# Rotary keys carried in the rows of the cache pages, and copied to their partitions by GpSimd

## The reference

```
s_past = (q_lat . ckv_past + q_rope . kr_past) * ATTN_SCALE     # 16 heads, 4096 positions
p      = softmax([s_past, s_new])
o      = p[past] . ckv_past + p[new] . c_kv
```

## Time and profile before

| | us |
|---|---|
| median of 3 runs | 932.12 (930.16 to 932.34) |
| the profiled execution | 928.51 |
| its span | 926.8 |
| TensorE busy in it | 885.7 (96%) |
| VectorE busy | 482.8 (52%) |
| ScalarE busy | 247.0 (27%) |
| GpSimd busy | 145.5 (16%) |

### The profile page before, as it was taken

How to read it: one execution, slowest core, us unless ns; L and a number is a source line. 1 busy time by engine, 2 the same in 40 slices (tenths; PEclk the granted TensorE clock), 3 DMA queues, 4 the chain that set the end, 5 groups by cost and what they waited for, 6 DMA issues and landing times.

```text
span 926.8 us, 14793 instructions
## 1 busy us (share of the span) xinstructions
PE 885.7 (96%) x5217; PEld 531.5 (57%) x5217; DVE 482.8 (52%) x1093; ACT 247.0 (27%) x553; POOL 145.5 (16%) x242
## 2 busy tenths in 40 slices
PE   8999999999999999999999999899999889987997
PEld 6777777777777766556678545443333333333443
DVE  2343789978752267767666445761111211114784
ACT  1122221122244126656620111221111111002246
POOL 0423433434323000000000000011211101111000
PEclk9999999999999999999999999999999989999999
DMA  9977998999999520101341695639999999998601
GB/s 371 379 246 253 332 337 281 332 358 327 321 307 340 206 75 26 44 21 43 114 193 46 250 422 217 260 118 410 423 423 423 422 422 426 422 418 347 236 24 69
DMA packets 76178, 247.61 MB, mean 267 GB/s; under 512 B 15397, under 2 KB 22830, under 8 KB 67110
## 3 DMA queue, kind: packets, MB, share of 16 engines
q1 hardware_dynamic: 54422, 191.42, 53.8%
q0 software_dynamic: 16288, 35.29, 10.6%
q10 hardware_dynamic: 5392, 19.93, 6.0%
HBM read 240.98 MB, written 18.05 MB: 279 GB/s over the span
## 4 chain that ended last, share of the span: by engine, by line
PE 76%; DMA 13%; DVE 5%; ACT 2%; issue 2%; SPq 1%; DVEq 0%; ACTq 0%; POOLq 0%
PE ps L1068 12%; DMA arena<-in_wexp 10%; PE ps L1572 9%; PE ps L1019 8%; PE ps L1492 6%; PE ps L1416 4%; PE ps L1594 3%; PE ps L1127 3%; PE ps L1157 3%; PE ps L1242 3%; PE ps L1059 3%; PE ps L1697 2%; PE ps L1264 2%; PE ps L1206 2%; PE ps L1223 2%
## 5 line engine op out<-in xcount | busy, mean ns | idle before, releaser
L1068 PE MATMUL ps<-arena 128*128 128x260 f32 x544 | 125.4, 386 | 2.1 <-DMA arena<-in_xT 1.5
L1068 PEld LDWEIGHTS ps<-arena 128*128 128x128 f32 x544 | 101.4, 190 | 23.0 <-issue 4.5
L2118 DVE SCALAR_TENSOR_TENSOR arena<-arena,vec 128x512 f32<-128x512 f32 x120 | 81.8, 746 | 0.0
L1019 PE MATMUL ps<-arena 128*128 128x260 f32 x336 | 78.5, 387 | 0.1
L1594 PE MATMUL ps<-arena 128*64 128x512 f32 x288 | 68.0, 615 | 6.2 <-DMA arena<-in_wexp 6.2
L2989 POOL DMA_DIRECT2D arena<-in_kv x96 | 52.1, 544 | 132.5 <-issue 128.6
L2814 DVE TENSOR_TENSOR arena<-ps,arena 128x256 f32<-128x256 f32 x18 | 7.6, 425 | 124.1 <-ACT arena L1967 124.1
L1572 PE MATMUL ps<-arena 128*64 128x512 f32 x288 | 65.4, 608 | 4.8 <-DMA arena<-in_wexp 3.8
L1019 PEld LDWEIGHTS ps<-arena 128*128 128x128 f32 x336 | 62.1, 190 | 12.9 <-issue 3.7
L1572 PE MATMUL ps<-arena,con 128*64 128x512 f32 x288 | 64.0, 596 | 3.3 <-DMA arena<-in_wexp 3.3
L1492 PE MATMUL ps<-arena 128*128 128x512 f32 x128 | 58.0, 600 | 0.0
(11 more groups left out here) (424 smaller groups left out, 1363.7 us busy)
## 6 DMA issues: line engine op xcount, KB each, us to landing
arena<-in_wexp SPq DMA_DIRECT2D x26, 2048.0 KB, 27.0
arena<-in_kv SPq DMA_DIRECT2D x160, 256.0 KB, 8.7
arena<-in_wexp SPq DMA_DIRECT2D x36, 1024.0 KB, 27.7
arena<-in_kv POOLq DMA_DIRECT2D x96, 256.0 KB, 7.4
arena<-in_w ACTq DMA_DIRECT2D x35, 512.0 KB, 8.5
arena<-in_wexp SPq DMA_DIRECT2D x16, 512.0 KB, 8.6
arena<-in_wo SPq DMA_DIRECT2D x8, 512.0 KB, 4.7
arena<-in_w_out SPq DMA_DIRECT2D x4, 1024.0 KB, 7.6
```

What stands on the lines that cost most here:

```text
L1019: y = mm(ps[:, paired_bank(p, n), 0:TH], left(k), right(k), start=(k == 0), stop=(k == KD // 2 - 1))
L1068: y = mm(ps[:, b + h, 0:TH], w[:, k], xT[:, k, h * TH:(h + 1) * TH], start=(k == 0), stop=(k == KD - 1))
L2118: y = v.scalar_tensor_tensor(out=aT[:, c, 0:NPR], in0=win, scalar=wt, in1=aT[:, c, 0:NPR], op0=ALU.mult, op1=ALU.add)
```

## The change

The keys no longer have a tensor of their own. They lie in the page's rows, between the transposed and the plain latents, as 32 more floats a row: `REC` is 544 floats, 2176 bytes. In a page the keys of positions 32c to 32c + 31 stand in partitions 32c to 32c + 31, so that a page fills all 128 partitions, with the 32 values of a key along them. All key transfers are gone from SP and GpSimd, and SP's wait on `s_ks` with them.

The score matmuls contract over 128 partitions that hold four groups. For this, GpSimd copies a step's keys from `kvr` to `krr` with four copies, each 64 partitions of 256 floats; x chooses the half that is written, h the half that is read. The copies of step n wait until all 16 pages of the step have landed. GpSimd's order is now: copy the keys of step n-1, wait for `v_step` n-2, ask for six pages of step n. `k_step` waits for the four copies in front of its key matmuls, and these write their 128 columns in runs of 32 to all of the step's columns. `krr` is now a tensor beside the arena, which keeps its size, and the descriptor scratch of the program is set to 4096 bytes a partition.

```diff
-REC = 2 * P + KVL
+REC = 2 * P + P // 4 + KVL
...
-A_KR = A_KV + 2 * STEPS * REC
-A_END1 = A_KR + 2 * 4 * P
+A_END1 = A_KV + 2 * STEPS * REC
...
-        krr = at(A_KR, 2 * 4 * P).rearrange("p (s b n) -> p s b n", s=2, b=4)
+        krr = sb("krr", [P, 2 * 4 * P])[:].rearrange("p (s b u h i) -> p s b u h i", s=2, b=4, u=2, h=2)
...
             sp.wait_ge(s_con, 112)
             step_pages(0)
-            step_keys(0)
-            step_keys(1)
             sp.wait_ge(s_q4, 1)
             step_pages(1)
             for n in range(2, STEPS):
...
-                sp.wait_ge(s_ks, n - 1)
-                step_keys(n)
                 sp.wait_ge(s_vs, n - 1)
                 step_pages(n)
...
-                pe.wait_ge(s_kv[s], 32 * SPN * (n // 2 + 1))
-                pe.wait_ge(s_kvp[s], 32 * (STEPS - SPN) * (n // 2 + 1))
+                pe.wait_ge(s_kv[s], 16 * SPN * (n // 2 + 1))
+                pe.wait_ge(s_kvp[s], 16 * (STEPS - SPN) * (n // 2 + 1))
...
+                pe.wait_ge(s_kf, 4 * (n + 1))
                 for j in range(2):
                     for bb in range(4):
-                        y = mm(ps[32 * bb:32 * bb + 32, bank, j * P:(j + 1) * P], qrz[:, j, 4 * r + bb, :], krr[:, s, bb],
-                               start=False, stop=(j == 1))
+                        y = mm(ps[32 * bb:32 * bb + 32, bank, 0:2 * P].rearrange("p (u h j i) -> p j u h i", u=2, h=2, j=2)[:, j],
+                               qrz[:, j, 4 * r + bb, :], krr[:, s, bb], start=False, stop=(j == 1))
...
-                                   kvr[:, s, bb, 2 * x + u, 2 * P:REC], start=(u == 0), stop=(u == 1))
+                                   kvr[:, s, bb, 2 * x + u, 2 * P + 32:REC], start=(u == 0), stop=(u == 1))
...
             def step_keys(n):
-                pool.load(numbers, pages[0:1, STEPS * n + SPN:STEPS * (n + 1)])
-                for j in range(STEPS - SPN):
-                    pg = pool.snap(numbers[j], min_val=0, max_val=NPOOL - 1)
-                    pool.dma_start(page_keys(n, SPN + j), a["kr"][bass.ds(pg, 1)].rearrange("a p n -> (a p) n")
-                                   ).then_inc(s_kvp[n % 2], 16)
+
+                pool.wait_ge(s_kv[n % 2], 16 * SPN * (n // 2 + 1))
+                pool.wait_ge(s_kvp[n % 2], 16 * (STEPS - SPN) * (n // 2 + 1))
+                for x in range(SIDES):
+                    for h in range(2):
+                        gp.tensor_copy(krr[64 * x:64 * x + 64, n % 2, :, :, h],
+                                       kvr[64 * h:64 * h + 64, n % 2, :, 2 * x:2 * x + 2, 2 * P:2 * P + 32]).then_inc(s_kf, 1)
 
             pool.wait_ge(s_con, 112)
             step_pages(0)
-            step_keys(0)
-            step_keys(1)
             pool.wait_ge(s_q4, 1)
             step_pages(1)
+            step_keys(0)
             for n in range(2, STEPS):
-                pool.wait_ge(s_ks, n - 1)
-                step_keys(n)
+                step_keys(n - 1)
                 pool.wait_ge(s_vs, n - 1)
                 step_pages(n)
+            step_keys(STEPS - 1)
...
-    krT = ckr.transpose(0, 2, 1)
+    krT = ckr.reshape(NPOOL, 4, 32, ROPE).transpose(0, 1, 3, 2).reshape(NPOOL, P, 32)
...
-        "kv": np.concatenate([ckT, ckv], 2), "kr": krT,
+        "kv": np.concatenate([ckT, krT, ckv], 2),
...
-    nc = bacc.Bacc("TRN2", target_bir_lowering=False, num_devices=1)
+    nc = bacc.Bacc("TRN2", target_bir_lowering=False, num_devices=1, dynamic_dma_scratch_size=4096)
```

More of the change, by code:

```diff
@@ L704, in decoder_layer @@
         OV_SLOT, OV_LOADS = 0, sum(k % 3 == 0 for k in range(EPAIRS))
-        def page_keys(n, j):
-            b, u = divmod(j, 4)
-            return krr[32 * u:32 * u + 32, n % 2, b]
         def narrow(bank, rows, w, ready=None):
@@ L1233, in scores @@
                 if hh == 0:
-                    pe.wait_ge(s_kf, 4)
+                    pe.wait_ge(s_kf, 4 * STEPS + 4)
                     pe.wait_ge(s_cse, 1)
```

## The result

| | before | after |
|---|---|---|
| median of 22 runs, us | 929.77 (927.52 to 932.46) | 932.30 (929.88 to 935.18) |
| ratio after / before | | 1.0025 (95% interval 1.0014 to 1.0035) |
| span of the profiled execution, us | 926.8 | 930.5 |
| TensorE busy from 76 to 310 us, of 234 | 231.64 | 229.25 |

The change makes the kernel 2.3 us slower (0.0025 x 929.8; 1.3 to 3.3 by the interval). The forecast was +1.2 us, inside 0.3% of no change, and that is where the result lies. The median of before is 929.77 over 22 runs, where the three that the prediction had gave 932.12, so only the ratio is compared. All ratios here are of runs in the chip's fast state: one of the four executions of e7 (2601.86 us, its cause unknown) and one of the kernel before beside e11 and e12 (950.42 us) are left out.

What follows compares the result with a forecast made beforehand. It took TensorE and just-in-time pages to bound the cache steps. Terms of -0.3 (SP's queue), +0.2 (copies), +0.8 (GpSimd's wait) and +0.5 (busy VectorE) gave +1.2 us, 933.3 us, with a range of 929.5 to 946.

Steps and rivals of the forecast that it cites:

- What bounds the kernel: Cache steps, 76 to 310 us: TensorE and DMA nearly full, pages just in time, 0.0 to 3.3 us margin a step.
- The bytes: Page and key transfers: same 0.26 MB a step in fewer transfers, net 0; bounds -0.8 and +0.8 us a step.
- Rival C: DMA queues relieved of small transfers, TensorE's 2.36 us of idle time go: 929.8 us; over 0.3% faster, chance 0.10.
- SP's queue: SP loses 160 issues and its `s_ks` waits; step 8's pages asked for 3.0 us sooner; -0.3 us.
- GpSimd's copies: At each step's landing: four copies of 356 ns, 1.42 us, against 1.55 us of cover; +0.2 us in all.
- copies that meet a busy VectorE: GpSimd's copies in the cache steps: now and then they meet a busy VectorE; +0.5 us.
- GpSimd's wait: GpSimd's page requests move back 4.8 us behind the landing, last page 0.3 us later a step; +0.8 us in all.
- The key matmuls and the scratch: `k_step`'s matmuls writing in runs of 32: 0; smaller scratch holding GpSimd's requests back: a rival, +370 us, chance 0.02.
- Rival A: GpSimd's circle of request, landing, copies sets the step, 14.5 to 17.5 us a turn; up to +12.4 us, 944.5; chance 0.18.
- Rival B: GpSimd's copies wait out VectorE's taps, 4.4 us for four; +6.5 us, 938.6; chance 0.20.
- The signs: In the cache steps: rival B by copies of 0.7 us and more; forecast by at most 3.5 us waits ahead of `k_step`'s matmuls.

Runs made afterwards that it cites:

- e7: Against the changed kernel: every step's four copies are made twice and `k_step` waits for both sets; 1.0154 of the kernel before.
- e11: Against the changed kernel: ScalarE makes the copies, ahead of its waits for VectorE's sums, and GpSimd neither copies nor waits for landings; second measurement, 0.9997 of the kernel before.
- e12: The changed kernel as it is, measured again beside the kernel with ScalarE's copies; 1.0015 of the kernel before.
- e1: Against the changed kernel: no GpSimd copies and no wait for a landing, krr zeroed once, cached rotary keys left out; 0.9979 of the kernel before.
- e2: Against the changed kernel: the four copies gone, GpSimd's wait for the landing kept, cached rotary keys left out; 1.0000 of the kernel before.
- e8: Against the kernel before: only the descriptor scratch set to 4096 bytes a partition; 1.0019.
- e10: Against the kernel before: only the descriptor scratch set to 4096 bytes a partition, measured a second time; 0.9985.
- e4: Against the changed kernel: SP asks for all sixteen pages of a step and GpSimd only copies keys; 1.0010 of the kernel before.
- e3: Against the changed kernel: each copy is a memset of the same places, which reads no SBUF, with the same waits; 0.9993 of the kernel before.
- e6: Against the changed kernel: GpSimd asks for its six pages before it copies the previous step's keys; 1.0358 of the kernel before.

## Why the prediction was right, and where its sum was off

**What bounds the kernel**: right. Pages that land just in time set what TensorE loses, and 3.2 of the 3.7 us between the two profiles lie ahead of `k_step` 15, in the stretch that was read.

**The bytes**: 0 was right for the time (e1). The engines' busy share fell by 0.06 of 234 us, so the transfers were relieved, but no wait of TensorE went with it; e1 has even 2.9 us of them. Rival C had its mechanism and no price.

**SP's queue**: right in kind. SP asks for step 8's pages 1.2 us after `v_step` 6 instead of 4.2, but `v_step` 6 itself ends 2.1 us later (its `k_step` was the one with the waits above), so they leave at 176.25 instead of 177.17.

**GpSimd's copies**: the two terms of them (0.2 and 0.5) came out very differently. Undisturbed, a copy took 0.40 us where 0.356 had been worked out, and four took 1.77 with their gaps, not 1.42. But the cover was 1.75 us and not 1.55, and the key matmuls followed 0.05 us after the copies, not 0.2. The errors cancel, and the forecast's 0.1 us in a step without margin stands as 0.03 in step 14. The mis-sized term is the 0.5 us booked for copies that meet a busy VectorE. It had no working, and it stood for copies of 612 ns in the mean and for all of the 2.3 us that the key matmuls waited, in steps 3, 6 and 12.

**GpSimd's wait**: booked at +0.8, the largest term of the sum, measured at 0 to within 0.16% of the kernel before (e2; beside e1 up to 2.7 us stay open). Both of its parts were too dear. The 2.12 us between `v_step` and the first request were taken over whole behind the copies; it is 0.27 us or nothing there. The requests for steps 2 to 15 leave 5.0 us after `v_step` in the mean instead of 2.1, which is 2.9 us later and not 4.8. And GpSimd's pages did not become the last in every step: the copies of step 6 begin with SP's landing, and those of step 9 with GpSimd's, whose last request left at 200.7 and landed 10.3 us later, at 211.0, with the copies at 211.12.

**The key matmuls and the scratch**: 0, right. The 16 records of a step still take 0.62 to 0.65 us; e8 and e10 together give 1.000.

**Rival A** got the picture and not the cause. The circle is what the chain shows, and `k_step`s in the changed kernel stand (313.00 - 95.19) / 13 = 16.75 us apart, GpSimd's copies just as far. But e2 keeps the circle and loses nothing against the kernel before, and e4 breaks it and still has 2.1 us of waits for copies. A chain through it says what came last, not what a shorter wait would be worth.

**Rival B** is the mechanism that is there, at a third of its price (2.3 of 6.5 us). Four copies had been priced at 4.4 us; beside taps and other instructions with two operands they took 2.5 to 3.2, and 5.7 once. They were held up in ten steps, but seven of these had room: in steps 4, 7 to 11 and 13 the copies began 1.5 to 4.9 us ahead of `k_step`, where the margins that had been read in the kernel before were 0.0 to 3.3. What made this room wasn't separated; e3, whose key matmuls never wait, has 4.7 us of it in step 4 and 2.7 in step 8. B was refused the forecast for want of a row. The Trainium skill's rule ("SBUF — State Buffer", "Who interferes with whom") had it: the trace agrees, with 402 ns in the median and up to 4310 ns beside VectorE's two-operand taps, and e3 agrees with its further part, that an instruction of GpSimd that only writes isn't held up. The rule should have given B the larger chance. It wouldn't have given a better number: B's +6.5 us is farther from the +2.3 measured than the forecast's +1.2.

**The signs** that the prediction had named point to B as well: copies of 0.7 us and more with a wait ahead of the key matmuls, and 1.4 + 2.3 = 3.7 us of waits ahead of `k_step`'s matmuls, where it had allowed 3.5.

**The chances**: 0.50 for no change within 0.3% was kept; 1.0025 with its interval up to 1.0035 was near the edge of it, toward the side that had 0.40. The class was right partly by luck: two thirds of the booked +1.2 us stood for a wait that cost nothing that can be told, and the hold-up that made the loss had a guess for a price.

## What to carry to other kernels

Before a copy goes to GpSimd, look at what VectorE does at that time: if it runs instructions with two SBUF operands end on end, count each of the copy's instructions at VectorE's length and not at its own, and keep a case for much more. Set the landing of the last transfer beside the start of its reader, step by step. Work that is put between them is hidden up to that margin and the reader's own work ahead of the data (1.75 us here); what is longer is paid in full, as in step 6, where 3.2 us of copies at a margin of 0.04 us made the key matmuls 1.5 us late. A copy whose place in an in-order queue is wrong costs far more than a slow copy (1.019 against 1.0025, with the same copies in the right place at 0.998 to 1.000), the more so as its longest waits were followed by some microseconds at half the clock.

## What the runs showed of the hardware

A copy of GpSimd that reads SBUF is held up beside instructions of VectorE with two SBUF operands. Where the two take turns it comes out at 742 to 757 ns instead of 400, about a tap's 747, and the taps go up to 886 ns, 766 in the mean over all 120. Where they don't take turns it waits for the whole row of taps: 4310 ns beside seven taps without a gap and 4105 beside six (the changed kernel and e12), 2770 and 2677 beside four (e4, e6), each time ending 0.26 us after the last tap. So GpSimd isn't served between two back-to-back instructions as a matter of course, and the 0.75 us that rival B allowed for a turn was no upper bound. Why it gets its turn in step 10 and not in step 3, both beside taps without a gap, stays open. A memset of the same places took 302 to 333 ns throughout, and ScalarE's copy 414 ns beside the same taps.

GpSimd's transfers of 2176-byte rows landed as before: 7.8 us in the median against 7.4. SP's took 5.6 against 8.7, because GpSimd asks later and SP has the engines to itself first: over steps 3 to 15 SP's median is 9.0 us in e1, where GpSimd asks as early as before, and 5.2 in e2, where it waits.
